# Projection in five tiles a block instead of six, an early start for the closing split, and several reorderings in an encoder-layer kernel

## What is computed

```python
h = rmsnorm(x, norm_pre)
proj = einsum('bld,de->ble', h, w_in)      # 1024 -> 7704 columns, split among branches
# A: gated linear attention   B: causal pooling mixer   C: gated DeltaNet
# each branch output * silu(its gate path) -> projection to 1024
merged = gts[:, :, 0] * y_gla + gts[:, :, 1] * y_pool + gts[:, :, 2] * y_gdn
y = merged @ w_out
x = x + rmsnorm(y, norm_post)
```

## Time and profile before

| | |
|---|---|
| median of 3 runs | 2521.21 us (2517.78 to 2522.13) |
| the profiled execution, its own time | 2525.03 us |
| its span, first to last instruction | 2523.1 us |
| TensorE busy | 2446.3 us (97%) |
| DVE, POOL, ACT busy | 1101.1, 820.5, 692.9 us |
| TensorE matmul instructions | 15943 |
| mean granted TensorE clock | 0.983 |

### The profile page before, as it was taken

The page is one execution under the profiler, slowest core; times in us unless marked ns, Lnnn a source line. Parts: engine busy times, 40 slices in busy tenths (PEclk is TensorE's granted clock), DMA queues, the critical chain, the costliest instruction groups (busy, mean ns, idle before and its releaser), DMA issues. The chain is left out here.

```text
span 2523.1 us, 40394 instructions
## 1 busy us (share of the span) xinstructions
PE 2446.3 (97%) x15943; PEld 2314.1 (92%) x15943; DVE 1101.1 (44%) x1862; ACT 692.9 (27%) x1429; POOL 820.5 (33%) x711
## 2 busy tenths in 40 slices
PE   7999999999999999998999999999999979999998
PEld 7989999999999999997999998899999879999886
DVE  6620111224466563005666665566666444224332
ACT  6211111111155531112322333223332243213221
POOL 1212211211121121124654565545655213334222
PEclk9989999999999999999999999999999879999999
DMA  5213512101111221331243225442233355543443
GB/s 165 74 69 111 214 52 76 43 34 60 43 52 52 77 77 70 114 100 54 83 114 113 81 81 188 144 114 81 81 92 104 126 179 181 202 170 128 155 150 96
DMA packets 200145, 264.99 MB, mean 105 GB/s; under 512 B 16176, under 2 KB 175296, under 8 KB 194432
## 3 DMA queue, kind: packets, MB, share of 16 engines
q1 hardware_dynamic: 200064, 263.86, 32.4%
HBM read 164.54 MB, written 99.29 MB: 105 GB/s over the span
## 5 line engine op out<-in xcount | busy, mean ns | idle before, releaser
L178 POOL TENSOR_TENSOR w_hi<-w_raw,zero 128x1024 fp32r<-128x1024 f32 x77 | 148.3, 1927 | 1169.9 <-PE dense L348 826.6
L346 PE MATMUL dense<-h_hi_first,w_hi 128*128 128x352 f32 x1032 | 342.2, 332 | 0.6 <-POOL w_lo L180 0.6
L347 PE MATMUL dense<-h_lo_first,w_hi 128*128 128x352 f32 x1032 | 335.1, 325 | 0.0
L348 PE MATMUL dense<-h_hi_first,w_lo 128*128 128x352 f32 x1032 | 335.0, 325 | 0.0
L347 PE MATMUL dense<-h_lo_second,w_hi 128*128 128x352 f32 x1032 | 334.0, 324 | 0.0
L348 PE MATMUL dense<-h_hi_second,w_lo 128*128 128x352 f32 x1032 | 333.2, 323 | 0.0
L346 PE MATMUL dense<-h_hi_second,w_hi 128*128 128x352 f32 x1032 | 332.3, 322 | 0.0
L1368 PE MATMUL gate_bank<-h_hi_first,w_hi 128*128 128x352 f32 x768 | 276.5, 360 | 5.9 <-SPq L1283 5.1
L1368 PE MATMUL gate_bank<-h_hi_first,w_lo 128*128 128x352 f32 x768 | 249.6, 325 | 0.0
L1368 PE MATMUL gate_bank<-h_lo_first,w_hi 128*128 128x352 f32 x768 | 249.4, 325 | 0.0
L346 PEld LDWEIGHTS dense<-h_hi_first,w_hi 128*128 128x128 f32 x1032 | 195.8, 190 | 6.0 <-POOL w_lo L180 1.9
(11 more groups left out here) (237 smaller groups left out, 4658.9 us busy)
## 6 DMA issues: line engine op xcount, KB each, us to landing
w_raw<-in_w_in SPq DMA_DIRECT2D x77, 512.0 KB, 6.1
rows_then_inputs<-scratch_feat SPq DMA_DIRECT2D x16, 1856.0 KB, 9.1
scratch_feat<-row_y SPq DMA_DIRECT2D x28, 1056.0 KB, 4.9
gate<-scratch_gates SPq DMA_DIRECT2D x12, 2112.0 KB, 8.7
scratch_gates<-gate_row SPq DMA_DIRECT2D x96, 176.0 KB, 1.9
o_raw<-scratch_branch_out SPq DMA_DIRECT2D x6, 2112.0 KB, 12.9
scratch_merged<-merged SPq DMA_DIRECT2D x48, 176.0 KB, 1.8
rows_then_inputs<-in_x_prompt SPq DMA_DIRECT2D x16, 512.0 KB, 3.5
```

Of the source, the lines that this page charges most:

```text
L178: nc.gpsimd.tensor_tensor(self.hi[:, p], raw, zeros, ALU.add).then_inc(self.high_ready, 1)
L346: nc.tensor.matmul(out, w_hi[:, p, k], h_hi[:, k, cols], start=(k == 0), stop=False)
L347: nc.tensor.matmul(out, w_hi[:, p, k], h_lo[:, k, cols], start=False, stop=False)
L348: mm = nc.tensor.matmul(out, w_lo[:, p, k], h_hi[:, k, cols], start=False, stop=(k == KD - 1))
```

## The change

Eight things, in the order of the program.

1. The six projection tiles of 352 columns become five: four of 416 and a middle one of 448 that joins the last 224 columns of the first half of h to the first 224 of the second, read as one operand of two runs. PSUM banks alternate by (t + p) since five is odd. The opening's schedule goes by the new tiles.
2. In the convolution slots the sigmoid is issued after the third of five tiles and the squares after the fourth.
3. In the opening, norm_pre is fetched ahead of the constants.
4. At the start of the chunk phase the releases of h and of the gate banks come ahead of the row loads and of ACT's table load.
5. At the swap of h's halves, the first third is released ahead of the wait and store of the last gate row.
6. In the sample chunk, ACT and DVE split the closing phase's first two input quarters (of three) and weight block 0, behind the copy of `gla_k` and behind `U0`; buffers are laid out anew for it, and `block_under` moves by one. SP's waits at the end of the chunk phase go into the closing phase.
7. The loads of x for the first two token tiles wait for an earlier product.
8. The last token tile is normed and added in two halves, both on DVE, with a store for each half.

Cut to its core (other lines replace TILES and TW in the same manner):

```diff
@@ -181,6 +181,46 @@
                                 ALU.subtract).then_inc(self.split_ready, 1)
+PROJ_TILES = 5
...
+MIDDLE = PROJ_TILES // 2
+PROJ_W = 416
+MIDDLE_PART = HALF_TOKENS - MIDDLE * PROJ_W
+SIG_W = 2 * MIDDLE_PART
+def width(t):
+    return 2 * MIDDLE_PART if t == MIDDLE else PROJ_W
+def span(t, shift=0):
+    start = t * PROJ_W + (2 * MIDDLE_PART - PROJ_W if t > MIDDLE else 0) + shift
+    return slice(start, start + width(t))
+class Halves:
+    SIZE = KD * HALF_TOKENS
+    def __init__(self, words, row, starts):
+        self.words, self.row, self.starts = words, row, starts
+        self.halves = [words[:, at:at + self.SIZE].rearrange("p (k t) -> p k t", k=KD) for at in starts]
+    def __getitem__(self, n):
+        return self.halves[n]
+    def tile(self, k, t):
+        if t == MIDDLE:
+            at = self.starts[0] + k * HALF_TOKENS + MIDDLE * PROJ_W
+            step = self.starts[1] - self.starts[0] - MIDDLE * PROJ_W
+            return bass.AP(self.words[:, :].tensor, at, [[self.row, P], [step, 2], [1, MIDDLE_PART]])
+        half, start = (0, t * PROJ_W) if t < MIDDLE else (1, MIDDLE_PART + (t - MIDDLE - 1) * PROJ_W)
+        return self.halves[half][:, k, start:start + PROJ_W]
 def norm_width(t):
     return P if t < CHUNKS else NS_
...
+    todo = [(t, f, k) for t in range(PROJ_TILES) for f in range(2) for k in range(KD)]
     plan = []
     for j in range(CHUNKS + 1):
         now = []
-        while todo and len(now) < STEPS and j >= -(-(todo[0][0] + 1) * TW // P) - 1 + 2:
+        while todo and len(now) < STEPS and j >= -(-span(todo[0][0]).stop // P) - 1 + 2:
...
                         if ahead_of_tile is not None:
                             ahead_of_tile(t)
                         if t >= 2:
-                            pe.wait_ge(own[0], own[1] * TILES + (t - 1))
+                            pe.wait_ge(own[0], own[1] * PROJ_TILES + (t - 1))
                         elif before is not None:
-                            pe.wait_ge(before[0], before[1] * TILES + (TILES + t - 1))
-                        h_hi, h_lo = hi[t // 3], lo[t // 3]
+                            pe.wait_ge(before[0], before[1] * PROJ_TILES + (PROJ_TILES + t - 1))
+                        out = dense[:, (t + p) % 2, 0:width(t)]
                         for k in range(KD):
-                            cols = slice(t % 3 * TW, (t % 3 + 1) * TW)
-                            out = dense[:, t % 2, 0:TW]
-                            nc.tensor.matmul(out, w_hi[:, p, k], h_hi[:, k, cols], start=(k == 0), stop=False)
-                            nc.tensor.matmul(out, w_hi[:, p, k], h_lo[:, k, cols], start=False, stop=False)
-                            mm = nc.tensor.matmul(out, w_lo[:, p, k], h_hi[:, k, cols], start=False,
+                            nc.tensor.matmul(out, w_hi[:, p, k], hi.tile(k, t), start=(k == 0), stop=False)
+                            nc.tensor.matmul(out, w_hi[:, p, k], lo.tile(k, t), start=False, stop=False)
+                            mm = nc.tensor.matmul(out, w_lo[:, p, k], hi.tile(k, t), start=False,
                                                   stop=(k == KD - 1))
                         mm.then_inc(dense_ready, 1)
...
-                        for t in (2 * tile, 2 * tile + 1):
+                        for t in range(2 * tile, min(2 * tile + 2, PROJ_TILES)):
...
-                            nc.tensor.matmul(side[:, t % 2, 0:TW], ones, T[:, t * TW:(t + 1) * TW],
+                                pe.wait_ge(norm_free, j * PROJ_TILES + (t - 1))
...
+                    for t in range(PROJ_TILES):
+                        if normed is not None:
+                            for u in range(2 * t, min(2 * t + 2, PROJ_TILES)):
+                                norm_logs(j - 2, u, 1 - p)
+                        if normed is not None and 2 * t + 1 == PROJ_TILES:
...
+                        act.wait_ge(dense_ready, j * PROJ_TILES + (F_CONV * PROJ_TILES + t + 1))
+                        write(t, dense[:, (t + p) % 2, 0:width(t)])
+                        if t == 2 and not (isinstance(j, int) and j == 0):
                             at_least(act, qkv_ready, j - 1)
                             conv_sigmoid(j - 1, 1 - p)
-                        if t == 4 and square:
+                        if t == 3 and square:
                             squares(j - 1, 1 - p)
...
+                sp.dma_start(gain[:, :], d["norm_pre"].to_broadcast([P, DM])).then_inc(gain_landed, 16)
                 sp.dma_start(consts[:, :], d["consts"]).then_inc(consts_landed, 16)
-                sp.dma_start(gain[:, :], d["norm_pre"].to_broadcast([P, DM])).then_inc(gain_landed, 16)
...
+                for a, b in ((0, 1), (2, 3), (4, 4)):
+                    at = slice(span(a).start, span(b).stop)
+                    store(gates[:, n, at], Y[:, 0, at], act_free, (A_GATE + n) * PROJ_TILES + b + 1, gate_stored[0])
...
+                def good(t):
+                    sp.wait_ge(h_landed[t], 2 * 16)
+                    sp.sem_inc(h_good[t], CHUNKS // 2)
...
+                            good(0)
                         sp.wait_ge(gate_taken, c * TILES + (T + 3))
...
+                for t in range(3):
+                    sp.sem_inc(h_good[t], CHUNKS // 2)
...
-                for t in range(3):
-                    sp.sem_inc(h_good[t], CHUNKS // 2)
...
-                for t in range(3):
+                for t in range(1, 3):
                     if t == 2:
                         outputs(CHUNKS // 2 - 1, 1)
-                    sp.wait_ge(h_landed[t], 2 * 16)
-                    sp.sem_inc(h_good[t], CHUNKS // 2)
+                    good(t)
...
-                sp.wait_ge(out_stored, 16 * (CHUNKS + 2))
-                sp.wait_ge(outg_stored, 16 * (CHUNKS + 2))
-                for q in range(2):
-                    sp.wait_ge(gate_stored[q], 16 * (LATE_GATES * TILES // 2 + 1))
...
+                    if then is None:
+                        before(act, "outg_ready", c)
+                        early_split.high(act, nc, late)
...
+                act.sem_inc(gate_taken, 2)
                 use_log_exp_tables(nc)
                 act.wait_ge(eps_ready, 1)
                 preload(act, ACT_)
-                act.sem_inc(gate_taken, 2)
...
+                    else:
+                        early_split.low(dve, nc, late)
...
+        act.wait_ge(late.o_landed, 16)
+        nc.scalar.copy(self.o_hi[0][:, :, :], late.o_raw[:, 0:4]).then_inc(self.o_high, 1)
+        act.wait_ge(late.wo_landed[0], 16)
+        nc.scalar.copy(self.wo_hi[:, :, :], late.wo_ring[:, 0]).then_inc(self.wo_high, 1)
+        nc.scalar.copy(self.o_hi[1][:, :, :], late.o_raw[:, 4:8]).then_inc(self.o_high, 1)
+    def low(self, dve, nc, late):
+        def difference(lo, raw, hi):
+            return nc.vector.tensor_tensor(lo[:, :, :], raw, hi[:, :, :].bitcast(F32), ALU.subtract)
+        dve.wait_ge(self.o_high, 1)
+        difference(self.o_lo[0], late.o_raw[:, 0:4], self.o_hi[0]).then_inc(self.o_split, 1)
+        dve.wait_ge(self.wo_high, 1)
+        difference(self.wo_lo, late.wo_ring[:, 0], self.wo_hi).then_inc(self.wo_split, 1)
+        dve.wait_ge(self.o_high, 2)
+        difference(self.o_lo[1], late.o_raw[:, 4:8], self.o_hi[1]).then_inc(self.o_split, 1)
...
-            return ((row + 1) * ROW - 1) // (4 * K * P)
...
                         next_wo(2)
                         next_wo(3)
+                        sp.wait_ge(late.out_stored, 16 * (CHUNKS + 2))
+                        sp.wait_ge(late.outg_stored, 16 * (CHUNKS + 2))
...
+                sp.wait_ge(y_ready, LAST * KD + 1)
                 load_x(0, 0)
...
-                store(CHUNKS, 0, NS_)
-                sp.wait_ge(stored[0], 16 * (CHUNKS // 2 + 1))
+                for half in range(2):
+                    at = slice(half * 512, half * 512 + 512)
+                    sp.wait_ge(last_ready, 1 + half)
+                    sp.dma_start(d["y_sample"][:, at], result[0:NS_, 0, at]).then_inc(stored[0], 16)
+                sp.wait_ge(stored[0], 16 * (CHUNKS // 2 + 2))
                 sp.wait_ge(stored[1], 16 * (CHUNKS // 2))
...
+                    if n < P:
+                        dve.wait_ge(x_landed[p], (CHUNKS // 2 + 1) * 16)
+                        dve.wait_ge(stored[p], CHUNKS // 2 * 16)
+                        for half in range(2):
+                            at = slice(half * 512, half * 512 + 512)
+                            nc.vector.scalar_tensor_tensor(normed[0:n, p, at], tokens_bank(p)[0:n, at], better,
+                                                           gain[0:n, at], ALU.mult, ALU.mult).then_inc(normed_ready, 1)
+                            dve.wait_ge(normed_ready, t + 1 + half)
+                            nc.vector.tensor_tensor(result[0:n, p, at], normed[0:n, p, at], x_in[0:n, p, at],
+                                                    ALU.add).then_inc(last_ready, 1)
+                        return
```

(4 more changed lines are left out.)

335 lines of the change are left out of this document (173 added, 162 removed).

## The result

The changed kernel takes 2508.09 us (median of 5 runs, 2506.64 to 2508.62) against 2521.21 (2517.78 to 2522.25): ratio 0.9946, 95% interval 0.9935 to 0.9956. I had forecast 2496.7, in a range from 2488 to 2507. The sign was right; the gain is 13.1 us where I summed up 24.5.

The account below looks back on a forecast made before the run. TensorE, busy throughout the projection and token tiles, was taken as the bound. Terms -15.4 - 5.4 + 3.0 + 0 + 0 - 4.8 - 1.9 = -24.5 us took the median from 2521.21 to 2496.7, range 2488 to 2507.

Parts of the forecast that it names:

- Five tiles, -15.4: Projection's 45 blocks: 1080 matmuls fewer at 14.3 ns each, columns unchanged, save 15.4 us; bounds 14.4 and 16.4.
- The rival of 2.5 ns: Projection: fixed cost per matmul is only 2.5 ns, so five tiles give 2.7 us, kernel 2509.4; chance 0.04.
- The second run: Middle projection tile's second run: priced at nothing; as rival, 92 ns per matmul, 99.7 us, kernel 2596; chance 0.04.
- float32 matmuls into `side`: Projection: these matmuls keep their columns with five tiles, so nothing is gained.
- Slots, -5.4: Convolution slots: TensorE's seven waits of 0.77 us for ACT's squares go, -5.4 us; bounds 0 and -6.
- Opening, +3.0: Opening: tile 0 needs four turned token tiles instead of three, first product later; net +3.0 us, bounds +1.5 and +5.
- Start of the chunk phase, 0: Earlier releases gain the first gate product up to 0.9 us, but DVE's chain is met next: 0, bounds -0.9 and 0.
- swap of h, 0: TensorE starts 1.8 us sooner but waits longer for the third release behind SP's issues: 0, bounds -3.5 and +1.8.
- Chunk to closing phase, -4.8: Splits moved into the sample chunk and SP's wait gone let TensorE start closing sooner: -4.8 us, bounds -2.4 and -5.6.
- The rival that the split doesn't fit: Sample chunk: inputs land later, ACT holds U, and the early split's gain halves, kernel 2499.2; chance 0.08.
- the one of the late squares: Convolution slots: ACT's order uses up the 0.5 us to spare, waits stay, kernel 2502.1; chance 0.12.
- Last tile, -1.9: Last token tile: halves on DVE end 1.0 us sooner and half the bytes land 0.9 sooner, -1.9; bounds -1 and -2.6.

Follow-up runs that it names:

- the stream alone: Only the projection's matmuls, all else left out of the kernel: 189.1 ns at 416 columns, 448 columns 202.3 in one run and 204.6 in two.
- six_tiles: Changed kernel with six projection tiles of 352 columns again, and sigmoid and squares back after the fourth and fifth tile: 2518.34 us.
- six_early: Changed kernel with six projection tiles of 352 columns again, sigmoid and squares kept after the third and fourth tile: 2511.9 us.
- split_undone: Changed kernel with ACT's copies and DVE's subtractions of the early split back at the start of the closing phase: 2513.01 us.

## Why the prediction failed, point by point

- **Five tiles, -15.4: the step that failed.** It was the split of a matmul's time from two rows: (226.3 - 160.3) / 160 columns = 0.412 ns a column, the rest, 14.3 ns, paid "per matmul whatever its width", and this line used for the widths between. It said 0.187 and 0.200 us for 416 and 448 columns, which makes a block of 22.75 us. The kernel has 188.8 and 203.6 ns and a block of 23.01. The extra over N / 2.4 ns (N the number of columns, 2.4 GHz the higher level of the clock) is not the same at every width: 13.8 ns at 352 columns, 15.5 at 416, 16.9 at 448. So 144 x 13.8 = 1.99 us a block became 96 x 15.5 + 24 x 16.9 = 1.89, which is the 0.10 us that was measured. 45 such blocks are 4.5 us (4.2 ns for each of the 1080 matmuls), where I had 15.4.
- **What was wrong with the line.** A part is the place. 512 columns cost 226.7 ns only where rows and starts are multiples of 64 words, as in the closing phase; `h` has rows of 1056, and there 512 columns cost 232.1. The line through 352 and 512 columns of such rows, 0.450 ns a column, gives 188.9 and 203.3 ns, as the kernel has. But other rows would not have saved it, for the widths don't lie on a line: from rows 1024 words apart the slope between 352 and 512 columns is my 0.41 and that between 256 and 512 is 0.416, and the widths between lie above. The extra over N / 2.4 there is 13.7 ns at 256 columns, 14.4 at 352, 15.0 at 416, 15.9 at 448, 16.7 at 480 and 13.3 to 13.6 at 512. My 14.3 ns, and the 13.3 of the nominal split, are near what 352 columns in the kernel and 512 in the closing phase have (13.8 and 13.3 to 13.6); two rows could not show what lies between. How much of the shortfall is place and how much width isn't told apart exactly, since a start alone moves 352 columns by a nanosecond or two as well. Why the extra grows from 352 to 480 columns and is gone at 512 stays open.
- **The rival of 2.5 ns** gave 2509.4, a microsecond from the result, and had 0.04 from me. That it came so near is luck. By its source, the Trainium skill (TensorE: Matmul & The Clock Gate, "Wait — 56ns, not 53.3ns?"), a warm matmul takes N / 2.4 + 2.5 ns: 149.2 ns at 352 columns and 175.8 at 416, where the traces have 160.5 and 188.8. The measurement decides: the rule does not hold for this stream, and the five tiles give little because wider matmuls have a larger extra, not because the extra is small.
- **The second run**, priced at nothing with 92 ns as the rival, costs 0.8 ns in the kernel's trace and 2.3 in the stream alone; either number holds a change of the start too.
- **float32 matmuls into `side`**, priced at nothing, are not clear. The three blocks that hold the forget gates took 84.9 us together before and in both kernels with six tiles, and 82.7 in the first profile of the changed kernel, but 84.4 in its second and 82.7 to 84.6 in the others with five; 0.3 of that are the dense tiles'. Where they are short, the first `project` is mostly late, so this trades against the opening. The four blocks of the pooling mixer are 0.4 us shorter in all beyond their dense tiles. It wasn't tried by itself.
- **Slots, -5.4**: right, 5.35 in the profiles of `six_tiles` and `six_early` (5.9 over the seven blocks alone), 6.4 in their medians. The layout worked out tile by tile held too: squares ended before the square sum was due.
- **Opening, +3.0**: right for the tiles, in the mean of several profiles. From the first turn to the first `project` it was 73.7 us before and 73.7 and 74.1 in the two kernels with six tiles; with five tiles and six steps it is 77.8 and 76.4 in the two profiles of the changed kernel and 76.9 in the mean of five, so about +3, from single executions that differ by 2.2. The first product came 18.60 after the first turn, where it was 14.59 before and 15.3 and 14.9 with six tiles; I had worked out 3.3 more. What I had not forecast is that the first turn itself came 2.8 sooner (10.73 to 7.94), so the first product started at 26.54 and not near 28.6. In all nine profiles with `norm_pre` fetched first, the first turn starts between 7.8 and 8.4. Whether the order does that, or before's one profile had a late fetch, stays open: it wasn't tried.
- **Start of the chunk phase, 0, and swap of h, 0**: right as far as it can be told. From the chunk phase's first matmul to the start of its second pass (TensorE's first wait of 0.41 for `Z`) it was 48.0 us before and is 47.0 and 46.6 in the changed kernel, but 46.9 to 49.2 in other profiles with the same edit (53.2 in the one where DVE stood). At the swap one wait went from 3.04 to 1.23, the other from 2.02 to 4.07, both as forecast.
- **Chunk to closing phase, -4.8**: from TensorE's last group of chunk matmuls to the first closing one it went from 13.60 to 7.99 us, and the rest of the closing phase is 0.4 longer, where TensorE now stands 0.91 before output block 6 (I had forecast over 1, and 0.8 given back): -5.2 in this pair of profiles, 4.6 to 4.9 by the medians of `split_undone`. The rival that the split doesn't fit is out, as is the one of the late squares.
- **Last tile, -1.9**: from the last matmul to the span's end 11.1 us became 10.0, so -1.1. DVE ended at 2500.57, 5.7 after the last matmul, where POOL's sum had ended about 6.7 after it: the 1.0 that I priced. From the last result to the end it is 4.3 us where it was 4.4: the half store gave 0.1 to 0.2 and not 0.9.

In medians, the parts shown by experiments are 3.8 (tiles with opening), 6.4 (slots) and 4.7 (split), with some 1.1 for the last tile: 16.0, above the 13.1 measured. `six_tiles` is only 3.3 us under before, where split and last tile should give 5.8. So 2 to 3 us are unaccounted for, about as much as the sum of several medians can be off. The pair of profiles gives 18.3 us instead: 11.1 up to the chunk phase (2.8 of them ahead of the first turn), 6.4 in it and up to the first closing matmul, and 1.1 at the end, less the 0.4 in the closing phase.

## What to carry to other kernels

To price fewer, larger matmuls, measure the very widths that the change will have, from the same operand and the same places. A slope taken between two stages of a kernel mixes width with layout, and even between like rows a line through two widths did not hold for those between them: at 416 and 448 columns it was off by 1 and 2 ns, and 2 to 4 ns in the kernel were enough to use up most of the gain. Where a whole block can be had at two numbers of matmuls, that difference is the price. And when a change moves one signal ahead of its queue's work, look at once at the next signal behind it: here that one, with the loads of the next chunk behind it instead of ahead, was worth another 5.9 us, and with it the kernel (2502.6 us) beats both versions.

## What the runs showed of the hardware

- A matmul of 512 columns takes 226.7 ns when the moving rows and starts lie at multiples of 64 words, 229.0 to 233.2 ns otherwise. For 480 columns the distance of the rows makes 1.4 ns (216.7 and 218.1). For 416 it makes 0.6 ns, and the start within rows 1056 words apart 1.3 ns (187.8 and 189.1). Why 416 columns with nothing moving still take 188.3 ns stays open.
- The time of a matmul over N / 2.4 ns depends on its width: with rows 1024 words apart it is 13.7 ns at 256 columns, 14.4 at 352, 15.0 at 416, 15.9 at 448, 16.7 at 480, and 13.3 to 13.6 at 512.
- Narrow matmuls, each with its weight load, have a floor of 111 ns: 111.1 at 128 columns, 111.6 at 132 and 176, then 119.5 at 256 and 121.5 at 264. Nothing was measured between 176 and 256.
- Two tiny operations of DVE took 6.79 us in one of two profiles of one kernel and 1.02 in the other, while POOL worked beside them in both. The Trainium skill (SBUF — State Buffer, Terms) says that DVE and GpSimd share a port pair and the loser blocks fully; a stand beside POOL's work would go with that, but in this one it outlasted several of POOL's operations, and no run separates it from other causes.
